# Nine shared weight buffers with the low half in place of the raw piece, and modulation gains spread by transposes

## The chip, the cores and the metric

The kernel runs on one core of one Trainium2 chip. The metric is the device time of one execution in microseconds (us), the median of several runs. Five engines work side by side, each in the order of its own program: TensorE (PE; its weight loads are shown apart, as PEld), VectorE (DVE), ScalarE (ACT), GpSimd (POOL), and SyncE (SP), which here only issues DMAs. They meet at semaphores alone. "Granted clock" is the share of full speed at which TensorE is allowed to run: it is either 1.00 or 0.50 in this trace.

## The reference

256 tokens of width 1024 go through two blocks of two layers each, all in float32. The first block has sparse attention, a gating branch, a gated feed-forward network and layer norms. The second is modulated: a vector `c` makes, through `ada_w`, six vectors for each layer, of which `g1` and `g2` (called gains here) multiply what a sublayer adds to the residual.

```python
def second_block(x, c, positions, ada_w, ada_b, norm_mix, norm_mlp, mlp_w1, mlp_w2, ...):
    cond = jax.nn.silu(c.astype(jnp.float32)).astype(x.dtype)
    for layer in range(DEPTH):
        mod = cond @ ada_w[layer] + ada_b[layer]
        sh1, sc1, g1, sh2, sc2, g2 = jnp.split(mod, 6, axis=-1)
        h = modulate(rms_norm(x, norm_mix[layer]), sh1, sc1)
        if layer % 2 == 0:
            y = even_mixer(h, ...)
        else:
            y = odd_mixer(h, ...)
        x = x + g1[:, None, :] * y
        h = modulate(rms_norm(x, norm_mlp[layer]), sh2, sc2)
        x = x + g2[:, None, :] * squared_relu_mlp(h, mlp_w1[layer], mlp_w2[layer])
    return x
```

## The kernel before, in words

**Weights.** All weight matrices lie in one array `W`, cut in 258 pieces of at most 128 partitions x 2048 float32 (1 MB); a list `seq` holds them in the order of use. 210 pieces are matmul weights. Each is loaded to one of three buffers `RAW`. ScalarE rounds it to the high half `WH` (line 1476, part `split`), VectorE subtracts to get the low half `WL` (line 1678), and TensorE makes each product as three: high x high, low times high activations, high times low activations (lines 1358 to 1360). `WH` and `WL` have three buffers each, a pair for a piece. So three pieces can be split ahead of the matmuls (`NPAIR`), and three loaded ahead of the splits (`NRAW`). The other 48 pieces are `ada_w_2`; VectorE reads them straight out of `RAW` and sums them into `ACC` (line 1737), in the slack of other work.

**When a piece is loaded.** SP issues the loads in the order of `seq`. Load n waits until `RAW` buffer n mod 3 is free: until VectorE has made the low half of piece n-3 (event `wl`), or has summed it (event `ada`). A split of a piece waits until it has landed, and until the last matmul of the piece that used the pair before (event `mm`).

**Order.** One Python pass writes a list of parts (`do(...)`), and each engine's program is that list with the other engines' parts left out. Generators (`linear`, `linear2`, `partial`, `weave`) place elementwise work between the slots of a matmul chunk; `advance` puts the next splits into the list wherever it is called. `busy(b, n)` (line 1343) issues n matmuls of constants: work whose result is thrown away, put ahead of a place where TensorE is to wait.

**Gains.** `modc` holds the modulation vectors as columns: 128 values down the partitions, one column per 128 channels. For the residual they are needed along the free dimension, the same in every partition, as `VG` (part of the tile `VEC`). Part `gain` makes 512 channels of it: VectorE multiplies the identity by four columns to get four diagonal blocks (line 2038, into `SQ` in the even layer and into `E` in the odd one), TensorE issues three filler matmuls and one fp32 matmul of ones by that buffer (line 1423), and ScalarE copies the result to `VG`. There are four gains in each layer of the second block, eight in all, woven between the matmul chunks of the mixer's first products.

Of the kernel before, what the change touches and what calls it, by code (L numbers as in the profile page):

```python
# [19 lines left out]
NRAW = 3  # L20
NPAIR = 3
# [157 lines left out]
def program(nc, W, xd, xTd, pTd, posd, pos2d, colvd, cstd, cstbd, vecd, sgwd, smalld, out):  # L179
    with ExitStack() as ctx:  # L180
# [35 lines left out]
        trig = sb("trig", [128, 4, 2, 40])  # L216
# [72 lines left out]
        for n, it in enumerate(seq):  # L289
            it["id"] = n  # L290
            it["freed"] = ("ada", (n, 3)) if it["name"] == "ada_w_2" else ("wl", n)
        cur = {"chunk": 0, "item": 0, "made": 0, "used": 0, "acc": 0, "sum": 0, "id": 0, "col": 0, "turn": 0, "buf": 0,
               "ada": None}
        pair_user = [None] * NPAIR
# [7 lines left out]

        def advance(most=NPAIR):
            while cur["item"] < len(seq) and most:
                it = seq[cur["item"]]
                if it["name"] == "ada_w_2":
# [3 lines left out]
                    do("ada", it, [] if it["a"] else acc_free[a])  # L310
                    if it["a"]:
# [36 lines left out]
        def linear(name, lhs, after, evac, touter=False, mid=None, guard=None, pad=(0, 0)):  # L348
# [5 lines left out]
            def slot(it, t):  # L354
# [3 lines left out]
                if t:  # L358
                    cur["used"] += 1

            if touter:
                assert len(its) <= NPAIR
# [31 lines left out]
        def linear2(name, lhs, after, evacs, mid, pad=(0, 0)):  # L394
# [13 lines left out]
            for t in range(2):  # L408
                if t:
                    ps[0][1], ps[1][1] = take(), take()  # L410
                for it in ia:
                    slot(it, 0, t)
                    if t:
                        cur["used"] += 1
# [8 lines left out]
            cur["used"] += 1  # L423
# [4 lines left out]
            cur["used"] += 1  # L428
# [9 lines left out]
        def partial(name, parts, ps, first, last, evac=None):  # L438
# [5 lines left out]
            def one(n, t):  # L444
# [4 lines left out]
                if t:  # L449
                    cur["used"] += 1  # L450
# [6 lines left out]
            else:  # L457
                assert len(its) <= NPAIR
# [46 lines left out]
        sq = {"free": []}  # L505
# [98 lines left out]

        advance(1)
# [274 lines left out]
        def gain(layer, k, hf, buf, box):  # L880
# [5 lines left out]
            do("gain", g, layer, k, hf, buf, b, mod_w[(layer, 3 * k + 2)] + box["free"], fr, list(vg_free[k]))  # L886
            box["free"] = [("gain_mm", g)]
# [37 lines left out]
        for i in range(2):  # L925
# [9 lines left out]
            if i == 0:  # L935
# [58 lines left out]
                gs = [lambda k=k, hf=hf: gain(0, k, hf, SQ[:, :], sq) for k in range(2) for hf in range(2)]  # L994
# [41 lines left out]
            else:  # L1036
# [13 lines left out]
                def turn_qk(c, t, base, lst):  # L1050
# [4 lines left out]
                gs = [lambda k=k, hf=hf: gain(1, k, hf, E[:, k, hf * 512:hf * 512 + 512], e_box[k])  # L1055
                      for k in range(2) for hf in range(2)]
# [185 lines left out]
        def sync_program(eng):  # L1242
            on = Waits(eng)

            def load(n):
                it = seq[n]
# [3 lines left out]
                eng.dma_start(RAW[:, n % NRAW, 0:w], W[it["off"]:it["off"] + 128 * w].rearrange("(p w) -> p w", p=128)  # L1250
                              ).then_inc(*landed(f"raw{n % NRAW}", n))

            for n in range(NRAW):
                load(n)
            eng.dma_start(X[:, :, :], xd[0].rearrange("(t p) d -> p t d", p=128)).then_inc(*landed("x", 0))
            for n in range(NRAW, len(seq)):
                load(n)
            for part, args in order:
                if part == "store":
                    t, after = args  # L1260
                    for e in after:
                        on.wait_ge(*at(*e))
                    eng.dma_start(out[0, tok(t), :], X[:, t, :]).then_inc(*landed(f"out{t}", 0))
# [900 lines left out]
```

## Time and profile before

| | |
|---|---|
| median of 3 runs | 1469.46 us (1466.57 to 1469.95) |
| the profiled execution's own time | 1465.74 us |
| its span, first to last instruction | 1463.9 us |
| mean granted clock | 0.980 |
| VectorE, ScalarE, GpSimd busy | 948.0, 657.1, 108.7 us |
| bytes read from HBM | 267.75 MB, 184 GB/s over the span |

How to read it: busy time is the time in which an engine has an instruction under way; TensorE's ends are modelled, and a matmul's shown duration overlaps the next one's, so its true pace is read from the distance of two starts. A wait is named by the instruction that waited and by what released it. Rows with "xN" stand for N instructions.

### The profile page before, as it was taken

How to read it: one execution, taken by the hardware profiler on the slowest of the kernel's cores; microseconds unless marked ns; L12 is line 12 of the kernel's file. 1: busy time of each engine (PE TensorE's matmuls, PEld its weight loads, DVE VectorE, ACT ScalarE, POOL GpSimd, SP SyncE). 2: the span in 40 equal slices, each digit the busy share in tenths (PEclk: the TensorE clock that was granted, in tenths of full speed). 3: DMA queues.
4: the chain of work that ended last, by engine and by line, in shares of the span. 5: the costliest groups of instructions: out<-in, count | busy, mean ns of one | idle time of the engine just before them, and what ended most of it. 6: DMA issues, size and time to landing. Idle time of an engine off the chain costs nothing.

```text
span 1463.9 us, 16616 instructions
## 1 busy us (share of the span) xinstructions
PE 1364.7 (93%) x6723; PEld 1111.9 (76%) x6723; DVE 948.0 (65%) x1257; ACT 657.1 (45%) x886; POOL 108.7 (7%) x156
## 2 busy tenths in 40 slices
PE   6899999999989999999799898999998978899998
PEld 5767888887867788887588776888876656688886
DVE  4856777766675677775566856867665775544444
ACT  4644533333554443333455444544435444454542
POOL 1010000000020000000222300000003130000000
PEclk9999999999999999999999999999999998999999
DMA  8505678763623688874143204776753330345551
GB/s 330 201 18 201 224 295 293 297 245 113 244 73 103 230 292 298 297 288 133 61 164 125 86 20 154 287 263 255 278 211 128 131 115 25 120 172 176 186 184 58
DMA packets 40236, 269.87 MB, mean 184 GB/s; under 512 B 4544, under 2 KB 4688, under 8 KB 11872
## 3 DMA queue, kind: packets, MB, share of 16 engines
q1 hardware_dynamic: 37712, 259.31, 49.3%
q0 software_dynamic: 2304, 8.46, 1.6%
q8 instruction: 53, 0.87, 0.2%
q10 hardware_dynamic: 144, 1.05, 0.2%
q14 instruction: 23, 0.19, 0.0%
HBM read 267.75 MB, written 1.05 MB: 184 GB/s over the span
## 4 chain that ended last, share of the span: by engine, by line
PE 72%; DVE 14%; ACT 6%; issue 3%; DMA 2%; POOL 2%; SPq 0%; DVEq 0%; ACTq 0%; POOLq 0%
PE ps L1358 21%; PE ps L1360 21%; PE ps L1359 21%; PE ps L1383 4%; DVE WL L1678 3%; DMA RAW<-W 2%; ACT WH L1476 2%; ACT E L1476 1%; PE ps L1371 1%; PE ps L1463 1%; POOL st L1282 1%; PE ps L1439 1%; DVE st L1872 1%; PE ps L1343 1%; ACT XTH L1476 1%
## 5 line engine op out<-in xcount | busy, mean ns | idle before, releaser
L1678 DVE TENSOR_TENSOR WL<-RAW,WH 128x2048 fp32r<-128x2048 f32 (+5 forms) x210 | 453.3, 2161 | 281.1 <-ACT WH L1476 280.9
L1358 PE MATMUL ps<-WH,XTH 128*128 128x512 f32 (+3 forms) x1176 | 459.3, 391 | 33.7 <-DVE XTL L1683 14.4
L1476 ACT ACTIVATE WH<-RAW 128x2048 fp32r<-128x2048 f32 (+5 forms) x210 | 379.9, 1810 | 245.8 <-PE ps L1360 217.1
L1360 PE MATMUL ps<-WH,XTL 128*128 128x512 f32 (+3 forms) x1176 | 447.6, 381 | 0.0
L1359 PE MATMUL ps<-WL,XTH 128*128 128x512 f32 (+3 forms) x1176 | 446.5, 380 | 0.0
L1358 PEld LDWEIGHTS ps<-WH,XTH 128*128 128x128 f32 x1176 | 222.3, 189 | 78.5 <-DVE XTL L1683 14.7
L1360 PEld LDWEIGHTS ps<-WH,XTL 128*128 128x128 f32 x1176 | 221.9, 189 | 38.6
L1359 PEld LDWEIGHTS ps<-WL,XTH 128*128 128x128 f32 x1176 | 222.6, 189 | 36.8 <-issue 1.9
L1358 PE MATMUL ps<-WH,HTH 128*128 128x512 f32 (+1 forms) x452 | 180.1, 398 | 3.2 <-DVE HTL L1759 3.2
L1359 PE MATMUL ps<-WL,HTH 128*128 128x512 f32 (+1 forms) x452 | 179.1, 396 | 0.0
L1360 PE MATMUL ps<-WH,HTL 128*128 128x512 f32 (+1 forms) x452 | 178.9, 396 | 0.0
L1737 DVE SCALAR_TENSOR_TENSOR ACC<-RAW,colv,ACC 128x512 f32<-128x512 f32 x168 | 126.1, 751 | 5.1
L1476 ACT ACTIVATE HTH<-ps 128x512 fp32r<-128x512 f32 (+1 forms) x58 | 32.1, 585 | 160.5 <-PE ps L1383 160.4
L1358 PEld LDWEIGHTS ps<-WH,HTH 128*128 128x128 f32 x452 | 86.2, 191 | 22.8 <-DVE HTL L1759 3.7
L1360 PEld LDWEIGHTS ps<-WH,HTL 128*128 128x128 f32 x452 | 86.2, 191 | 19.8
L1359 PEld LDWEIGHTS ps<-WL,HTH 128*128 128x128 f32 x452 | 86.4, 191 | 19.2
L1280 POOL TENSOR_SCALAR st<-st 128x1 f32<-128x1 f32 (+3 forms) x42 | 21.6, 513 | 1034.5 <-DVE st L1943 540.1
L1476 ACT ACTIVATE GB<-ps 128x512 f32<-128x512 f32 (+1 forms) x94 | 46.3, 499 | 88.3 <-PE ps L1360 88.2
L1476 ACT ACTIVATE E<-ps,st 128x128 f32<-128x128 f32 (+1 forms) x104 | 42.4, 420 | 79.8 <-DVE st L1882 79.8
L1343 PE MATMUL ps<-cstb 128*128 128x512 bf16 x283 | 78.1, 398 | 0.0
L1759 DVE TENSOR_TENSOR HTL<-ps,HTH 128x512 fp32r<-128x512 f32 x54 | 35.8, 687 | 37.7 <-ACT HTH L1476 37.7
L1282 POOL TENSOR_TENSOR st<-st,cst 128x1 f32<-128x1 f32 (+3 forms) x42 | 47.2, 1124 | 3.5
(177 smaller groups left out, 1063.5 us busy)
## 6 DMA issues: line engine op xcount, KB each, us to landing
RAW<-W SPq DMA_DIRECT2D x220, 1024.0 KB, 4.8
RAW<-W SPq DMA_DIRECT2D x7, 960.0 KB, 4.7
RAW<-W SPq DMA_DIRECT2D x6, 910.0 KB, 6.2
RAW<-W SPq DMA_DIRECT2D x9, 576.0 KB, 3.5
VEC<-vecd POOLq DMA_DIRECT2D x10, 512.0 KB, 6.0
RAW<-W SPq DMA_DIRECT2D x8, 512.0 KB, 3.4
RAW<-W SPq DMA_DIRECT2D x6, 546.0 KB, 4.4
GB<-xTd ACTq DMA_DIRECT2D x1, 1024.0 KB, 8.3
```

The lines of the kernel that those rows point to most:

```text
L1280: eng.tensor_scalar(x, x, scale, eps, ALU.mult, ALU.add).then_inc(*own.up())
L1282: eng.tensor_tensor(x, x, MH.to_broadcast([128, x.shape[1]]), ALU.pow).then_inc(*up("rsqrt", key))
L1343: eng.matmul(banks[b][:, :], identb, cstb[:, 0:512], start=True, stop=True)
L1358: eng.matmul(ps, xh, hi[:, j, c0:c0 + cw], start=first and j == 0, stop=False)
L1359: eng.matmul(ps, xh, lo[:, j, c0:c0 + cw], start=False, stop=False)
L1360: op = eng.matmul(ps, xl, hi[:, j, c0:c0 + cw], start=False, stop=last and j == n - 1)
L1371: op = eng.matmul(banks[b][:, q:q + 1], ACC[:, a, q * 128:q * 128 + 128], ones[:, 0:1], start=True, stop=True)
L1383: op = eng.transpose(banks[b][0:rows, j * 128:j * 128 + 128], src, ident)
L1476: return eng.activation(dst, src, f, **k)
L1678: eng.tensor_tensor(WL[:, p, 0:w], RAW[:, n % NRAW, 0:w], WH[:, p, 0:w].bitcast(F32), ALU.subtract).then_inc(*up("wl", n))
L1737: op = eng.scalar_tensor_tensor(out=ACC[:, a, :], in0=view[:, j, :], scalar=cond[:, kt:kt + 1], in1=ACC[:, a, :], op0=ALU.mult, op1=ALU.add)
L1759: eng.tensor_tensor(HTL[:, r2:r2 + 2, :], banks[b][:, :].rearrange("p (n q) -> p n q", n=2), HTH[:, r2:r2 + 2, :].bitcast(F32), ALU.subtra ...
```

## The change

It has two parts.

**Buffers.** `RAW`, `WH` and `WL` become one pool of nine buffers of the same size `WB` (seen as float32 under the name `RAW`). A load takes the buffer at the head of a queue of free ones, and so does the high half of a split; the low half is written over the raw piece itself. After the last matmul of a piece its two buffers go to the end of the queue with the event `mm`; an `ada_w_2` piece gives back its one with the event `ada`. The limits stay: three pairs, and three pieces loaded but not yet split. The loads, which SP had in a loop of their own, now stand in the common list of parts. `trig`, used once at the start, moves into `SQ`.

**Gains.** The diagonal on VectorE, the three fillers and the matmul of ones are gone. In their place TensorE transposes, four times, a column of `modc` that is read 128 times over (a step of 0), with the identity as the moving operand: each gives a block of 128 x 128 in which every row holds the 128 values.

```diff
-        RAW = sb("RAW", [128, NRAW, SLOT])
-        WH = sb("WH", [128, NPAIR, SLOT], F32R)
-        WL = sb("WL", [128, NPAIR, SLOT], F32R)
+        with nc.sbuf_tensor("RAW", [128, NBUF, SLOT], F32) as RAW:
+            pass
+        WB = sb("WB", [128, NBUF, SLOT], F32R)
...
-        trig = sb("trig", [128, 4, 2, 40])
+        trig = SQ[:, 0:320].rearrange("p (n t f) -> p n t f", n=4, t=2)
...
+        def loads(most=NBUF):
+            while cur["load"] < len(seq) and most and cur["load"] - cur["item"] < NBUF - 2 * cur["pairs"] and bufs:
+                it = seq[cur["load"]]
+                it["raw"], after = bufs.pop(0)
+                do("load", it, after)
+                cur["load"] += 1
+                most -= 1
+
+        def advance(most=NBUF):
+            loads()
+            while cur["item"] < cur["load"] and most:
                 it = seq[cur["item"]]
                 if it["name"] == "ada_w_2":
...
                     do("ada", it, [] if it["a"] else acc_free[a])
+                    bufs.append((it["raw"], [("ada", (it["id"], 3))]))
...
                 else:
-                    if cur["made"] - cur["used"] >= NPAIR:
+                    if cur["ahead"] >= cur["pairs"] or not bufs:
                         return
                     most -= 1
-                    p = it["pair"] = cur["made"] % NPAIR
-                    cur["made"] += 1
-                    do("split", it, pair_user[p])
-                    pair_user[p] = it["id"]
+                    cur["ahead"] += 1
+                    it["high"], after = bufs.pop(0)
+                    do("split", it, after)
                 cur["item"] += 1
+                loads()
+
+        def used(it):
+            cur["ahead"] -= 1
+            for b in (it["high"], it["raw"]):
+                bufs.append((b, [("mm", it["id"])]))
+            loads()
...
         def sync_program(eng):
...
-                if n >= NRAW:
-                    on.wait_ge(*at(*seq[n - NRAW]["freed"]))
+                for e in after:
+                    on.wait_ge(*at(*e))
...
-            def gain(g, layer, k, hf, buf, b, _, fr, __):
-                for e in fr:
-                    on.wait_ge(*at(*e))
-                busy(b, 3)
-                on.wait_ge(*at("diag", g))
-                eng.matmul(banks[b][:, :], ones, buf, start=True, stop=True).then_inc(*up("gain_mm", g))
+            def gain(g, layer, k, hf, b, after, fr, _):
+                for e in fr + after:
+                    on.wait_ge(*at(*e))
+                on.wait_ge(*at("cst", 0))
+                for j in range(4):
+                    c = 24 * k + 16 + hf * 4 + j
+                    op = eng.transpose(banks[b][:, j * 128:j * 128 + 128],
+                                       modc[:, layer, c:c + 1].to_broadcast([128, 128]), ident)
+                op.then_inc(*up("gain_mm", g))
...
-                eng.tensor_tensor(WL[:, p, 0:w], RAW[:, n % NRAW, 0:w], WH[:, p, 0:w].bitcast(F32), ALU.subtract
-                                  ).then_inc(*up("wl", n))
+                eng.tensor_tensor(WB[:, it["raw"], 0:w], RAW[:, it["raw"], 0:w], WB[:, it["high"], 0:w].bitcast(F32),
+                                  ALU.subtract).then_inc(*up("wl", n))
...
-            def gain(g, layer, k, hf, buf, b, after, _, __):
-                c0 = 24 * k + 16 + hf * 4
-                on.wait_ge(*at("cst", 0))
-                for e in after:
-                    on.wait_ge(*at(*e))
-                eng.tensor_tensor(buf.rearrange("p (a n) -> p a n", a=4), ident.unsqueeze(1).broadcast_to([128, 4, 128]),
-                                  modc[:, layer, c0:c0 + 4].unsqueeze(2).broadcast_to([128, 4, 128]), ALU.mult
-                                  ).then_inc(*up("diag", g))
```

TensorE's program at the first gain of the even layer before the change, between two chunks of `even_w_in_2` (`cstb` holds the constants of the fillers, `SQ` the diagonal):

```order
L1359 MATMUL ps<-WL,XTH 128x384
L1360 MATMUL ps<-WH,XTL 128x384
L1343 MATMUL ps<-cstb 128x512 x3
L1423 MATMUL ps<-SQ,cst 128x512
L1358 MATMUL ps<-WH,XTH 128x384
L1359 MATMUL ps<-WL,XTH 128x384
```

And the same place in the change (its lines have other numbers, and both halves are called `WB`):

```order
L1376 MATMUL ps<-WB,XTH 128x384
L1377 MATMUL ps<-WB,XTL 128x384
L1442 MATMUL ps<-cst,modc 128x128 x4
L1375 MATMUL ps<-WB,XTH 128x384
L1376 MATMUL ps<-WB,XTH 128x384
```

Three fillers and a matmul of 512 columns give way to four transposes of 128; nothing else moves on TensorE, here or at the seven other gains, and VectorE loses the eight diagonals and nothing more.

SP's program at its start, with the semaphores that each load waits for, before (`s_wl` is raised by VectorE's low half):

```order
L1250 DMA RAW<-W 128x1820
L1255 DMA X<-xd 128x2x1024
L1250 DMA RAW<-W 128x1092 [waits s_wl]
L1250 DMA RAW<-W 128x1820 [waits s_wl]
L1250 DMA RAW<-W 128x1092 [waits s_wl]
L1250 DMA RAW<-W 128x2048 [waits s_wl] x8
```

And in the change (`s_mm` is raised by TensorE's last matmul of a piece):

```order
L1266 DMA RAW<-W 128x1820
L1270 DMA X<-xd 128x2x1024
L1266 DMA RAW<-W 128x1092
L1266 DMA RAW<-W 128x1820
L1266 DMA RAW<-W 128x1092
L1266 DMA RAW<-W 128x2048 [waits s_mm] x8
```

The loads keep their order. The fourth to the sixth wait for nothing now, and from the seventh on a load waits for matmuls that are further back, in place of a low half that comes later. ScalarE's program, with all its splits, keeps its order and its waits.

## Rows read from the trace of the kernel before

**Rows 1.** The page, part 1: busy time, share of the span and instructions of each engine.
```profile
PE 1364.7 (93%) x6723; PEld 1111.9 (76%) x6723; DVE 948.0 (65%) x1257; ACT 657.1 (45%) x886; POOL 108.7 (7%) x156
```

**Rows 2.** Waits of TensorE: who <- whom: us in total, times, longest.
```profile
PE ps L1439 <- DVE selb L1860: 4.4, 2, 2.7
PE ps L1423 <- DVE E L2038: 2.6, 2, 1.3
PE ps L1358 <- DVE WL L1678: 2.4, 3, 1.1
...
PE ps L1423 <- DVE SQ L2038: 1.0, 1, 1.0
```

**Rows 3.** Stretches: length, busy PE, PEld, DVE, ACT, POOL, clock, DMA share, GB/s.
```profile
23.00:27.00 4.00, 4.00 (x26) 4.00 (x25) 1.94 (x4) 3.53 (x6) 2.24 (x5) 1.00 0.23 67
...
421.00:427.60 6.60, 5.05 (x20) 3.67 (x21) 4.04 (x10) 3.37 (x17) 1.15 (x1) 0.50 0.00 0
750.00:785.00 35.00, 33.96 (x181) 29.36 (x180) 30.58 (x42) 18.21 (x24) 9.28 (x8) 1.00 0.45 152
784.00:788.00 4.00, 3.61 (x33) 3.36 (x31) 1.45 (x3) 3.39 (x7) 0.00 (x0) 1.00 0.69 240
1125.00:1160.00 35.00, 32.36 (x135) 23.30 (x134) 27.49 (x34) 16.86 (x18) 11.27 (x8) 1.00 0.49 177
```

**Rows 4.** One line's instructions: the diagonals, ns min/median/max of one.
```profile
L2038 DVE TENSOR_TENSOR SQ<-cst,modc x4: 680/684/684, 759.2 to 778.7; 128x512 f32<-128x512 f32 x4
```

**Rows 5.** TensorE in order of time at the first gain: start, us, line, tiles.
```profile
759.62 0.82 PE L1343 MATMUL ps<-cstb 128*128 128x512 bf16 x3
760.28 1.02 PE L1423 MATMUL ps<-SQ,cst 128*128 128x512 f32 x2
...
761.32 0.34 PE L1359 MATMUL ps<-WL,XTH 128*128 128x384 f32 x1
761.49 0.34 PE L1360 MATMUL ps<-WH,XTL 128*128 128x384 f32 x1
```

**Rows 6.** TensorE in order of time at the eighth gain.
```profile
1154.75 0.82 PE L1343 MATMUL ps<-cstb 128*128 128x512 bf16 x3
...
1158.07 0.40 PE L1359 MATMUL ps<-WL,XTH 128*128 128x512 f32 x1
```

**Rows 7.** TensorE in order of time: eight transposes between weight matmuls.
```profile
946.08 1.03 PE L1383 MATMUL ps<-cst,GB 128*128 128x128 f32 x8
...
947.18 0.40 PE L1359 MATMUL ps<-WL,XTH 128*128 128x512 f32 x1
947.41 0.39 PE L1360 MATMUL ps<-WH,XTL 128*128 128x512 f32 x1
```

**Rows 8.** VectorE in order of time where the two stretches of gains end.
```profile
785.46 0.69 DVE L1751 COPY T<-ps 96x512 f32<-96x512 f32 x1 [1.39 <-PE ps L1383]
...
1164.38 0.69 DVE L1751 COPY T<-ps 128x512 f32<-128x512 f32 x1 [1.61 <-PE ps L1383]
```

**Rows 9.** SP in order of time: issue of the seventh load.
```profile
26.83 0.33 SPq L1250 DMA_DIRECT2D RAW<-W  x1
```

**Rows 10.** TensorE in order of time: the first piece's last matmul.
```profile
23.06 0.34 PE L1360 MATMUL ps<-WH,XTL 128*128 128x364 f32 x1
```

**Rows 11.** ScalarE in order of time: the seventh and eighth pieces.
```profile
36.66 1.92 ACT L1476 ACTIVATE WH<-RAW 128x2048 fp32r<-128x2048 f32 x1 [3.22 <-DMA RAW<-W]
40.09 1.92 ACT L1476 ACTIVATE WH<-RAW 128x2048 fp32r<-128x2048 f32 x1 [1.51 <-DMA RAW<-W]
```

**Rows 12.** VectorE in order of time: low half, first rotation.
```profile
42.04 2.29 DVE L1678 TENSOR_TENSOR WL<-RAW,WH 128x2048 fp32r<-128x2048 f32 x1 [1.14 <-ACT WH L1476]
44.24 0.23 DVE L1795 TENSOR_TENSOR SCR<-H,COS 128x80 f32<-128x80 f32 x1
```

**Rows 13.** TensorE in order of time behind those rotations, first and second layer.
```profile
49.08 0.63 PE L1383 MATMUL ps<-cst,H 128*128 128x128 f32 x4 [0.52 <-DVE MIX L1819]
...
393.19 1.65 PE L1404 MATMUL ps<-T 64*128 64x128 f32 x16 [0.56 <-DVE T L1751]
```

More of the change, by code:

```diff
@@ L19 @@
 SLOT = 2048
-NRAW = 3
-NPAIR = 3
+NBUF = 9
 DFF = 2816
@@ L290, in program @@
             it["id"] = n
-            it["freed"] = ("ada", (n, 3)) if it["name"] == "ada_w_2" else ("wl", n)
-        cur = {"chunk": 0, "item": 0, "made": 0, "used": 0, "acc": 0, "sum": 0, "id": 0, "col": 0, "turn": 0, "buf": 0,
+        cur = {"chunk": 0, "item": 0, "load": 0, "ahead": 0, "pairs": 3, "acc": 0, "sum": 0, "id": 0, "col": 0, "turn": 0, "buf": 0,
                "ada": None}
-        pair_user = [None] * NPAIR
+        bufs = [(n, []) for n in range(NBUF)]
         acc_free = [[], []]
@@ L358, in slot @@
                 if t:
-                    cur["used"] += 1
+                    used(it)
             if touter:
-                assert len(its) <= NPAIR
+                assert len(its) <= cur["pairs"]
                 advance()
@@ L422, in linear2 @@
                 slot(ib[0], 1, t)
-            cur["used"] += 1
+            used(ib[0])
             yield
@@ L427, in linear2 @@
                 slot(ib[1], 1, t)
-            cur["used"] += 1
+            used(ib[1])
             for t in range(2):
@@ L449, in one @@
                 if t:
-                    cur["used"] += 1
+                    used(it)
             if evac is None:
@@ L457, in partial @@
             else:
-                assert len(its) <= NPAIR
+                assert len(its) <= cur["pairs"]
                 advance()
@@ L504, in program @@
         scr = {"free": [("cstb", 0)]}
-        sq = {"free": []}
+        sq = {"free": [("trig", 0)]}
         def weave(gen, steps):
@@ L601, in normalised @@
             return dict(n=nh, done=done)
+        loads(3)
+        do("load_x")
         advance(1)
@@ L878, in program, with gain @@
         vg_free, vg_w = [list(vec_free[0]), list(vec_free[0])], [[], []]
-        def gain(layer, k, hf, buf, box):
+        def gain(layer, k, hf):
             assert len(mod_w[(layer, 3 * k + 2)]) == 2
@@ L885, in gain @@
             b, fr = take()
-            do("gain", g, layer, k, hf, buf, b, mod_w[(layer, 3 * k + 2)] + box["free"], fr, list(vg_free[k]))
-            box["free"] = [("gain_mm", g)]
+            do("gain", g, layer, k, hf, b, mod_w[(layer, 3 * k + 2)], fr, list(vg_free[k]))
             vg_w[k].append(("gain", g))
@@ L993, in program @@
                                             SIN[:, t, 8:40:2], sm[nm], ww[t], E[:, n, :], e_box[n], mr[n, t])
-                gs = [lambda k=k, hf=hf: gain(0, k, hf, SQ[:, :], sq) for k in range(2) for hf in range(2)]
+                gs = [lambda k=k, hf=hf: gain(0, k, hf) for k in range(2) for hf in range(2)]
                 run(weave(dils(4, 5, 0), [[mch[0, 0][0], mch[1, 0][0]], [gs[0], mch[0, 0][1], mch[0, 1][0]],
@@ L1054, in program @@
                 e_box = [{"free": list(e_free[0])}, {"free": list(e_free[1])}]
-                gs = [lambda k=k, hf=hf: gain(1, k, hf, E[:, k, hf * 512:hf * 512 + 512], e_box[k])
-                      for k in range(2) for hf in range(2)]
+                gs = [lambda k=k, hf=hf: gain(1, k, hf) for k in range(2) for hf in range(2)]
                 run(weave(chain(linear2("odd_w_in_2", "x", xt_w, [put_H("odd", c, c * 512, c * 512 + 512, dw[c])
@@ L1478, in scalar_program, with split @@
             eng.dma_start(GBT, xTd.rearrange("p (k n) -> p k n", k=8)).then_inc(*landed("xT", 0))
-            def split(it, user):
-                n, p, w = it["id"], it["pair"], it["n"] * it["w"]
-                on.wait_ge(*at(f"raw{n % NRAW}", n))
-                if user is not None:
-                    on.wait_ge(*at("mm", user))
-                act(WH[:, p, 0:w], RAW[:, n % NRAW, 0:w], ACT.Copy).then_inc(*up("wh", n))
+            def split(it, after):
+                n, w = it["id"], it["n"] * it["w"]
+                on.wait_ge(*at(f"raw{it['raw']}", n))
+                for e in after:
+                    on.wait_ge(*at(*e))
+                act(WB[:, it["high"], 0:w], RAW[:, it["raw"], 0:w], ACT.Copy).then_inc(*up("wh", n))
             def x0(t):
@@ L1647, in qk_sq, with gain @@
                 act(sqt, x, ACT.Square).then_inc(*up("qk_sq", key))
-            def gain(g, layer, k, hf, buf, b, _, __, after):
+            def gain(g, layer, k, hf, b, _, __, after):
                 on.wait_ge(*at("gain_mm", g))
```

40 lines of the change are left out of this document (18 added, 22 removed).

## The prediction

> **What bounds the kernel now.** I read the page's busy times first: TensorE is busy in 93% of the span, VectorE in 65% [rows 1]. A shown matmul overlaps the next one, so the share alone proves little; the distance of starts does. Inside a chunk three-pass matmuls start 0.17 us apart at 384 columns [rows 5] and 0.23 us apart at 512 [rows 7], with nothing between them: TensorE is the bound there, and whatever it no longer does comes off the time unless another engine is close behind. Second, its waits [rows 2]: for the low half of weights it waits 2.4 us in all, so a freer weight pipeline has little to give as such; for the gains' diagonals it waits 2.6 + 1.0 = 3.6 us. Third, the stretches in which the gains lie, 750 to 785 us (four of the even layer) and 1125 to 1160 us (most of the four of the odd one) [rows 3]: TensorE is busy 33.96 and 32.36 of 35 us, VectorE 30.58 and 27.49. So TensorE leads there, and VectorE is the one close behind.
>
> **The gains, TensorE's part.** I time one old gain from the start of the fillers to the start that the next weight matmul would have had at its usual pace, which is the second weight matmul's start less one distance (the first shows its wait for the fp32 matmul in its own length). At the first gain [rows 5]: 761.32 − 0.17 − 759.62 = 1.53 us, without a wait: three fillers, then one fp32 matmul of 512 columns. At the eighth [rows 6]: 1158.07 − 0.23 − 1154.75 = 3.09 us, with the longest of the waits for a diagonal, 1.3 [rows 2]. Read so, the eight cost 1.53, 1.84, 2.79, 1.52, 1.51, 3.10, 1.59 and 3.09 us: 17.0 in sum. By the grouped rows it is 8 × 1.53 + 3.6 = 15.8; the missing 1.1 is what a late start adds to the pipeline's refill. I take 17.0 and keep 15.8 as a bound.
>
> What comes instead is four fp32 transposes of 128 columns. Eight of that form, between the same kind of weight matmuls, took 947.18 − 0.23 − 946.08 = 0.87 us [rows 7]: 0.11 each, 0.44 for four, 3.5 for all eight gains. The difference is 17.0 − 3.5 = 13.5 us. The new wait that the transposes bring, for `modc`, moves from VectorE to TensorE; the diagonal that had it ran at 759.2 us [rows 4], before the fillers were over, so it costs nothing. What the trace doesn't have is a stationary operand that reads one column 128 times. Upper bound: its four passes cost what the old fp32 matmul cost for the same 512 columns, from its start to the next one's pace, 761.15 − 760.28 = 0.87 us [rows 5]; that takes 8 × 0.43 = 3.4 us off the saving. Lower bound: the 0.44 itself, since a repeated column gives TensorE no fewer columns to pass than any other. I take 0.44, as form and size are those of [rows 7] and only the address step differs.
>
> The trace has 0.11 us for each of the transposes. By the Trainium skill (TensorE: Matmul & The Clock Gate, section on LDWEIGHTS) a load takes columns / 1.2 ns, whatever it reads, so an estimate by the page is 107 ns for 128 columns; it names no penalty for a step of 0, so it would leave the sum at 13.5, where the upper bound gives 10.1.
>
> **The gains, VectorE's part.** Eight diagonals of 0.68 us go [rows 4]: 2.7 us in each stretch. That counts only if VectorE becomes late. Two facts: in the even stretch TensorE saves 1.53 + 1.84 + 2.79 + 1.52 − 4 × 0.44 = 5.9 us, VectorE has 35 − 30.58 = 4.4 us idle and loses 2.7 of work: 7.1 of room [rows 3, 4]. In the odd one TensorE saves 9.29 − 1.76 = 7.5, VectorE has 7.5 idle and loses 2.7: 10.2 of room. And at the end of both the next copy of VectorE waited for TensorE, 1.39 and 1.61 us [rows 8]. So VectorE can follow; it could take up to 1 us of the even stretch, as its idle time isn't all in the right place. No other engine's order moves there; ScalarE has half of its time free.
>
> **The buffers.** There are nine buffers of 1 MB before and after. From the seventh load on, a load used to wait for a low half three pieces back; now it waits for the matmuls of a piece some six back, done earlier. The pieces land earlier, but TensorE waited only 2.4 us for low halves [rows 2], so I count a gain only where a late load reached TensorE through the splits. That is at the start. DMA's share is 0.23 from 23 to 27 us [rows 3], since SP issues the seventh load at 26.83 [rows 9]; the first piece's last matmul, for which it now waits, ends at 23.06 + 0.34 = 23.40 [rows 10]. So 3.4 us earlier. The seventh split waited 3.22 us for DMA, the eighth 1.51 [rows 11]; both waits go, so the eighth starts at least 1.5 us sooner, and with it VectorE's low half, which waited for it, and the rotations that stand right behind [rows 12]. TensorE's stalls behind those rotations are 0.52 and 0.56 us, with the refill 0.68 and 0.72 [rows 13], and I take 1.35 of these 1.40. The same stall in the second layer (393.19) [rows 13] should go by the same means, 0.7. Bounds: nothing at all, if other waits take their place at once; 3.2 + 0.7 + 2.4 = 6.3, if the whole wait of the seventh split comes through to the end of the layer's attention, where TensorE waits up to 2.7 us for VectorE's `selb` [rows 2], and the waits for low halves all go. I take 2.05.
>
> Loads four to six are issued some 10 us earlier. They stand in one queue behind the first three and X, so they overtake nothing.
>
> **Sum.** 13.5 + 2.05 = 15.5 us. The profiled execution took 1465.74 us for a span of 1463.9; less 15.5 it is 1450.2. The median of the runs shown stands 3.7 us above it (1469.46), so the time as measured is 1469.46 − 15.5 = 1454.0. The terms' own bounds: least 15.8 − 8 × 0.87 = 8.8, less 1 for VectorE, 7.8, so 1461.7; most 13.5 + 6.3 = 19.8, so 1449.7. The three runs spread over 3.4 us, so the forecast's own range is 1448 to 1462.
>
> **Rivals.**
> (B) *VectorE becomes the bound in both stretches.* For: 30.58 of 35 us busy in the even one [rows 3], and the diagonals came late at half of the gains [rows 2], so VectorE runs behind TensorE in places. Against: the copies at the ends wait for TensorE [rows 8]. Then only VectorE's relief counts: 8 × 0.68 + 2.05 = 7.5 us, 1462.
> (C) *The earlier loads give much more.* For: SP's late loads leave DMA idle in places. DMA's share is 0.45 and 0.49 in the gains' stretches [rows 3]. If both waits of [rows 11] came off in full (4.7 us), with the second layer's 0.7, the 2.4 for low halves and 1 more that no row names, the gain would be 22.3: 1447. Against: between them and the end stand TensorE's stalls of 0.68 and 0.72 us, which is all that it can take back there itself.
> (D) *The buffers give nothing*, because the splits come where their place in the program and the pair limit put them: 13.5 alone, 1456. It lies inside the range.
> (E) *Slower: the granted clock falls behind the gains.* TensorE's clock is 0.50 from 421.0 to 427.6 us, where it is busy 5.05 of 6.60 us [rows 3]; full speed is 2.4 GHz, so it is at 1.2 there. The fillers go at all eight gains. If each were followed by one such stretch, half of 6.6 us would be lost eight times, 26.4 us: 1454 + 26.4 = 1480. It decides from 15.5 / 8 = 1.9 us lost, or 3.9 us at low clock, behind each. Against: without fillers and waits TensorE is busier there, not idler; and from 784 to 788 us, where it makes the 32 transposes of keys and queries in a row, the clock stays at 1.00 [rows 3].
> For that rule stands the Trainium skill (TensorE: Matmul & The Clock Gate, section PE-mode transpose): the full clock "doesn't engage" for transposes, which don't count as busy. This trace disagrees for 3.5 us in a row, and here only 0.44 us of them stand between weight matmuls; no run yet shows them in the place of fillers.
>
> **How the numbers follow.** Forecast with (D) 0.80, (B) 0.11, (C) 0.04, (E) 0.03, and 0.02 for a change that moves nothing because something outside the gains' stretches sets the time. The range from 1447 to 1463 holds the first three, but for tails that I put at 0.1 together. About 0.3%, 4.4 us, is what a measurement of this kernel can tell from no change. The forecast, (C) and (D) are well beyond it; of (B) most is, since its 7.5 us could shrink by half if VectorE is late by more. So faster 0.92, within 0.3% 0.05, slower 0.03.
>
> **What would show it.** In the changed kernel's trace: at each gain the distance from the last weight matmul to the next one's pace is 0.4 to 0.5 us, with no wait named before the transposes. If it is 0.8, the repeated column is dear. The weight matmuls behind them keep their 0.17 and 0.23 us apart and clock 1.00; else (E). The copies of VectorE at the ends of both stretches still wait for TensorE, and the even stretch ends about 6 us, the odd one 7.5 us nearer to its beginning; else (B). The seventh load is issued near 23.4 us, the seventh split doesn't wait for DMA, and TensorE's stalls at 49 and 52 us are gone; else (D). I'd be wrong in kind if TensorE's waits elsewhere grew by what it saved here.

## The result and the profile after

| | before | changed |
|---|---|---|
| median of all runs taken together | 1468.01 us (4 runs, 1466.08 to 1469.95) | 1452.71 us (4 runs, 1450.07 to 1456.84) |
| ratio | | 0.9899, 95% interval 0.9882 to 0.9917 |
| profiled execution, its span | 1465.74, 1463.9 us | 1450.07, 1448.3 us |
| mean granted clock of it | 0.980 | 0.981 |

The forecast was 1454.0 us by a saving of 15.5. The two spans differ by 15.6 us, the medians by 15.3. Measured again beside before on the same chip, the changed kernel gave a ratio of 0.9892 (0.9874 to 0.9909).

The page of the changed kernel, parts 1 and 2 (busy time, share and instructions of each engine; granted clock in 40 slices):

```profile
PE 1352.1 (93%) x6683; PEld 1111.1 (77%) x6715; DVE 943.2 (65%) x1249; ACT 656.9 (45%) x886; POOL 113.7 (8%) x156
...
PEclk9999999999999999999999999999999988999999
```

TensorE's busy time fell by 12.6 us and VectorE's by 4.8 against [rows 1]: 8 diagonals of 0.68 make 5.4. The share of TensorE is what it was, since the span fell with it.

TensorE at the first and at the eighth gain, in order of time (start, us; lines have moved by 17, and both halves are `WB` now):

```profile
757.90 0.60 PE L1442 MATMUL ps<-cst,modc 128*128 128x128 f32 x4
758.25 0.42 PE L1375 MATMUL ps<-WB,XTH 128*128 128x384 f32 x1
758.51 0.34 PE L1376 MATMUL ps<-WB,XTH 128*128 128x384 f32 x1
...
1141.59 0.60 PE L1442 MATMUL ps<-cst,modc 128*128 128x128 f32 x4
1141.94 0.48 PE L1375 MATMUL ps<-WB,XTH 128*128 128x512 f32 x1
1142.26 0.39 PE L1376 MATMUL ps<-WB,XTH 128*128 128x512 f32 x1
```

Read as in the prediction: 758.51 − 0.17 − 757.90 = 0.44 us, and 1142.26 − 0.23 − 1141.59 = 0.44 us, where [rows 5, 6] give 1.53 and 3.09. No wait is named before the transposes.

The waits of TensorE in the changed kernel (who <- whom: us in total, times, longest):

```profile
PE ps L1460 <- DVE selb L1881: 4.4, 2, 2.7
...
PE ps L1375 <- DVE WB L1699: 2.4, 3, 1.1
```

The rows of [rows 2] for the diagonals are gone; those for the low half and for `selb` stand as they were. The pool did nothing for TensorE's waits for weights.

The start: SP's seventh load, ScalarE's seventh and eighth piece, and VectorE's first rotation in the changed kernel:

```profile
23.56 1.82 SPq L1266 DMA_DIRECT2D RAW<-W  x2
```
```profile
33.46 1.91 ACT L1497 ACTIVATE WB<-RAW 128x2048 fp32r<-128x2048 f32 x1
38.18 1.92 ACT L1497 ACTIVATE WB<-RAW 128x2048 fp32r<-128x2048 f32 x1 [2.81 <-PE ps L1377]
```
```profile
42.34 0.24 DVE L1816 TENSOR_TENSOR SCR<-H,COS 128x80 f32<-128x80 f32 x1
```

The load is issued 3.3 us sooner than in [rows 9]; both waits for DMA of [rows 11] are gone, and the eighth split now waits for the matmuls of the pair before; the rotation starts 1.9 us sooner than in [rows 12]. TensorE behind it, first and second layer:

```profile
48.26 0.60 PE L1400 MATMUL ps<-cst,H 128*128 128x128 f32 x4
...
50.23 1.65 PE L1421 MATMUL ps<-T 64*128 64x128 f32 x16
...
390.97 1.65 PE L1421 MATMUL ps<-T 64*128 64x128 f32 x16
```

The waits of [rows 13] are gone. VectorE's copies at the ends of the even and the odd stretch, which waited 1.39 and 1.61 us for TensorE in [rows 8]:

```profile
778.71 1.28 DVE L1772 COPY T<-ps 96x512 f32<-96x512 f32 x2
```
```profile
1148.57 0.69 DVE L1772 COPY T<-ps 128x512 f32<-128x512 f32 x1
```

Neither waits for TensorE any more, so VectorE has used up its room there. TensorE doesn't wait for VectorE at these ends either: it waits 0.82 and 0.93 us for a copy of ScalarE, where before it waited 0.82 and 0.94.

To find where the time came from, I compare when the same weight matmul starts in both traces, and call the difference the lead. All 4932 weight matmuls have a counterpart.

| place | forecast | lead gained |
|---|---|---|
| up to the first scores (before at 53 us) | 1.35 | 1.44 |
| second layer's scores (395 us) | 0.7 | 0.77 |
| from there to the first gain | 0 | −0.48 |
| the four gains of the even layer (lead 1.73 to 7.55) | 5.9 | 5.82 |
| between them and the odd layer's gains | 0 | 0.67 |
| the four gains of the odd layer (lead 8.22 to 15.81) | 7.5 | 7.59 |
| from there to the end | 0 | −0.20 |
| sum | 15.5 | 15.61 |

The three rows whose forecast is 0 hold steps of 0.3 to 2.7 us of both signs. The largest stand where one trace has a stretch at granted clock 0.50 and the other hasn't, or has it at another place (before's matmuls from 1086 to 1114 us: the lead rises by 2.7 and falls by 2.3). That the three rows cancel to 0.01 us is luck.

### The profile page after: what moved, and what is told of

It is laid out like the page before. It is cut to its first block, busy times and chain, and to the rows that moved or that the text cites. A ratio compares the mean times of both kernels' runs of the same rounds, so it can differ in the third digit from the quotient of the medians.

```text
span 1448.3 us, 16560 instructions
## 1 busy us (share of the span) xinstructions
PE 1352.1 (93%) x6683; PEld 1111.1 (77%) x6715; DVE 943.2 (65%) x1249; ACT 656.9 (45%) x886; POOL 113.7 (8%) x156
## 4 chain that ended last, share of the span: by engine, by line
PE 78%; DVE 11%; ACT 5%; issue 2%; POOL 2%; DMA 1%; DVEq 0%; ACTq 0%; POOLq 0%
PE ps L1375 23%; PE ps L1377 23%; PE ps L1376 23%; PE ps L1400 4%; DVE WB L1699 2%; ACT E L1497 1%; PE ps L1484 1%; PE ps L1388 1%; POOL st L1299 1%; ACT WB L1497 1%; PE ps L1460 1%; DVE st L1893 1%; PE ps L1360 1%; ACT XTH L1497 1%; DVE st L1961 1%
## 5 line engine op out<-in xcount | busy, mean ns | idle before, releaser
L1699 DVE TENSOR_TENSOR WB<-RAW,WB 128x2048 fp32r<-128x2048 f32 (+5 forms) x210 | 453.3, 2161 | 271.7 <-ACT WB L1497 271.5
L1375 PE MATMUL ps<-WB,XTH 128*128 128x512 f32 (+3 forms) x1176 | 457.3, 389 | 33.3 <-DVE XTL L1704 14.0
L1497 ACT ACTIVATE WB<-RAW 128x2048 fp32r<-128x2048 f32 (+5 forms) x210 | 379.8, 1809 | 237.5 <-PE ps L1377 223.1
L1377 PE MATMUL ps<-WB,XTL 128*128 128x512 f32 (+3 forms) x1176 | 447.9, 381 | 0.0
L1376 PE MATMUL ps<-WB,XTH 128*128 128x512 f32 (+3 forms) x1176 | 447.2, 380 | 0.0
L1375 PEld LDWEIGHTS ps<-WB,XTH 128*128 128x128 f32 x1176 | 222.7, 189 | 75.7 <-DVE XTL L1704 14.0
L1377 PEld LDWEIGHTS ps<-WB,XTL 128*128 128x128 f32 x1176 | 222.5, 189 | 38.7
L1376 PEld LDWEIGHTS ps<-WB,XTH 128*128 128x128 f32 x1176 | 223.0, 190 | 34.8
L1375 PE MATMUL ps<-WB,HTH 128*128 128x512 f32 (+1 forms) x452 | 179.3, 397 | 3.2 <-DVE HTL L1780 3.2
L1376 PE MATMUL ps<-WB,HTH 128*128 128x512 f32 (+1 forms) x452 | 178.5, 395 | 0.0
L1377 PE MATMUL ps<-WB,HTL 128*128 128x512 f32 (+1 forms) x452 | 178.5, 395 | 0.0
L1375 PEld LDWEIGHTS ps<-WB,HTH 128*128 128x128 f32 x452 | 85.9, 190 | 22.7 <-DVE HTL L1780 3.7
L1377 PEld LDWEIGHTS ps<-WB,HTL 128*128 128x128 f32 x452 | 85.8, 190 | 19.6
L1376 PEld LDWEIGHTS ps<-WB,HTH 128*128 128x128 f32 x452 | 86.0, 190 | 19.1
```

What stands on the lines that cost most here:

```text
L1375: eng.matmul(ps, xh, hi[:, j, c0:c0 + cw], start=first and j == 0, stop=False)
L1376: eng.matmul(ps, xh, lo[:, j, c0:c0 + cw], start=False, stop=False)
L1377: op = eng.matmul(ps, xl, hi[:, j, c0:c0 + cw], start=False, stop=last and j == n - 1)
L1497: return eng.activation(dst, src, f, **k)
L1699: eng.tensor_tensor(WB[:, it["raw"], 0:w], RAW[:, it["raw"], 0:w], WB[:, it["high"], 0:w].bitcast(F32), ALU.subtract).then_inc(*up("wl", n))
```

## Experiments

All ran beside before; the ratio is to before. The column "at 0.980" is explained under the clock and the runs' spread.

| kernel | ratio (95%) | median, runs | mean clock of the runs | at 0.980 |
|---|---|---|---|---|
| transposes alone | 0.9941 (0.9919 to 0.9962) | 1459.1 (6) | 0.976 | 1455.6 |
| nine buffers alone | 0.9985 (0.9975 to 0.9994) | 1465.4 (11) | 0.979 | 1464.2 |
| changed, loads at the old pace | 0.9924 (0.9903 to 0.9944) | 1455.1 (6) | 0.979 | 1454.7 |
| changed, diagonals kept unread | 0.9928 (0.9914 to 0.9942) | 1456.8 (5) | 0.978 | 1455.2 |
| nine buffers, old gains without fillers | 0.9989 (0.9979 to 0.9998) | 1467.7 (10) | 0.980 | 1466.9 |
| changed, three fillers put back | 0.9917 (0.9900 to 0.9933) | 1456.7 (4) | 0.981 | 1457.6 |
| changed, 20 transposes a gain | 1.0004 (0.9991 to 1.0017) | 1470.0 (10) | 0.977 | 1466.8 |
| the same with a full stationary tile | 0.9991 (0.9982 to 1.0001) | 1467.2 (10) | 0.978 | 1466.3 |
| changed, fewer fillers | 0.9893 (0.9877 to 0.9910) | 1451.2 (5) | 0.969 | |
| changed, no filler at all | 0.9952 (0.9937 to 0.9967) | 1460.8 (7) | 0.948 | |
| changed, fewer fillers at chosen places | 0.9842 (0.9826 to 0.9857) | 1445.6 (5) | 0.981 | 1446.6 |
| changed, once more | 0.9892 (0.9874 to 0.9909) | 1451.7 (6) | 0.980 | 1453.1 |

### The transposes alone

The kernel before with the new `gain` on TensorE; `RAW`, `WH`, `WL` and the loads' waits as before.

```diff
-                busy(b, 3)
-                on.wait_ge(*at("diag", g))
-                eng.matmul(banks[b][:, :], ones, buf, start=True, stop=True).then_inc(*up("gain_mm", g))
+                for j in range(4):
+                    c = 24 * k + 16 + hf * 4 + j
+                    op = eng.transpose(banks[b][:, j * 128:j * 128 + 128],
+                                       modc[:, layer, c:c + 1].to_broadcast([128, 128]), ident)
```

> The kernel before with the gains' transposes alone; the three pools and the load waits stay as before. Theory (the gains are 13.5 of the 15.5 us): 13.5 us below before, ratio 0.9908, each gain 0.44 us on TensorE; TensorE's stalls near 49 and 52 us and at 393 us stay. Rival (VectorE follows too slowly unless pieces come earlier): under 10 us, with VectorE's copies at the ends of the two stretches no longer waiting for TensorE.

Measured: 0.9941, 8.7 us, short of what was expected (0.9908 lies outside the interval). Both signs named for the rival are there: it is under 10 us, and VectorE's copies at the ends of the two stretches (783.91 and 1153.81 us) wait for TensorE no longer. Yet TensorE doesn't wait for VectorE there, but 0.82 and 0.94 us for ScalarE as in before, so the rival isn't what took the time. In the trace the gains gave what was forecast: the lead over before rises from −3.49 to 2.34 us over the even layer's four and from 2.99 to 10.58 over the odd layer's, 13.4 in sum. TensorE in order of time at one of them, and behind the first layer's rotations:

```profile
763.11 0.60 PE L1422 MATMUL ps<-cst,modc 128*128 128x128 f32 x4
763.47 0.42 PE L1356 MATMUL ps<-WH,XTH 128*128 128x384 f32 x1
763.73 0.34 PE L1357 MATMUL ps<-WL,XTH 128*128 128x384 f32 x1
```
```profile
48.95 0.63 PE L1381 MATMUL ps<-cst,H 128*128 128x128 f32 x4 [0.49 <-DVE MIX L1820]
...
51.55 1.65 PE L1402 MATMUL ps<-T 64*128 64x128 f32 x16 [0.56 <-DVE T L1752]
```

0.44 us a gain, and the old stalls. The rest, 5.7 us, was lost outside, in parts that this kernel shares with before, most of it at granted clock 0.50: this trace has 76 us of it, before's 60 and the changed kernel's 56. Its six runs reach from 1452.75 to 1463.10, with mean clocks from 0.982 to 0.971; the fastest lies 14 us under before's median beside it, 1466.98, and 12 under before's fastest. So what the transposes save in place is shown; whether this kernel draws a low clock more often than the others, or six runs fell so, stays open.

### The nine buffers alone

The changed kernel with the old gains: diagonal on VectorE (into `SQ` or `E`), three fillers, matmul of ones.

> The changed kernel with the gains as before (diagonal, three fillers, matmul of ones): the nine buffers alone. Theory: 2 us below before (ratio 0.9986, hard to tell from none by the times); in the trace the lead over before is 1.3 us behind the first layer's rotations and 0.75 more in the second layer, nothing elsewhere. Rival (the pool makes nothing): lead within 0.5 us all through. Rival (the pool helps the diagonals too): more than 4 us.

```profile
48.80 1.03 PE L1362 MATMUL ps<-cstb 128*128 128x512 bf16 x4
49.80 1.65 PE L1423 MATMUL ps<-T 64*128 64x128 f32 x16
```
```profile
759.08 0.82 PE L1362 MATMUL ps<-cstb 128*128 128x512 bf16 x3
759.73 1.02 PE L1443 MATMUL ps<-SQ,cst 128*128 128x512 f32 x2
760.19 0.74 PE L1377 MATMUL ps<-WB,XTH 128*128 128x384 f32 x1
760.77 0.34 PE L1378 MATMUL ps<-WB,XTH 128*128 128x384 f32 x1
```

TensorE in order of time: no stall before the scores, and an old gain of 760.77 − 0.17 − 759.08 = 1.52 us. The lead steps up by 1.56 us up to the first scores and by 0.8 in the second layer; the gains' stretches add nothing. The ratio, 0.9985, is 2.2 us. That is as expected. The two profiled spans differ by 0.6 us alone, since this trace loses 2.6 us between the two steps, at 80 and at 140 us, where its stretches at 0.50 stand elsewhere than before's.

### The changed kernel with the loads at their old pace

```diff
                 it["raw"], after = bufs.pop(0)
+                n = cur["load"] - 3
+                if n >= 0:
+                    after = after + [("ada", (n, 3)) if seq[n]["name"] == "ada_w_2" else ("wl", n)]
```

> The changed kernel, but each load waits besides for the low half (or the sum) of the piece three back, as before: nine buffers in name, the old pace of the loads. Theory (the small gain is the loads' earlier issue): 2 us slower than the changed kernel, ratio to before 0.991; TensorE's stalls near 49, 52 and 393 us are back. Rival (it comes from the splits or the place of the low half): as the changed kernel, ratio 0.9895, without those stalls.

```profile
27.00 3.04 SPq L1269 DMA_DIRECT2D RAW<-W  x2
```
```profile
49.24 0.63 PE L1403 MATMUL ps<-cst,H 128*128 128x128 f32 x4 [0.18 <-DVE MIX L1843]
...
51.84 1.65 PE L1424 MATMUL ps<-T 64*128 64x128 f32 x16 [0.56 <-DVE T L1775]
```

The seventh load is issued at 27.00 us again (SP's row), and TensorE stalls again behind the rotations. The lead of the changed kernel over this one grows by 1.0 us there and is 1.6 at the first scores, where this kernel is no further than before: the first layer's gain comes from the loads' issue. In the second layer the stall did not come back. There ScalarE's split still waits 1.80 us for DMA (2.47 in before, 0 in the changed kernel), so the piece is late but by 0.7 us less than in before, and the stall was no longer than that. Why it lands sooner with the waits of before is open. The ratio, 0.9924 beside 0.9892 to 0.9899, is 4 to 5 us more than the changed kernel's, and at equal clock it is 1.6 (1454.7 and 1453.1 in the table); the intervals of the two overlap, so the times alone don't tell this from no difference.

### The diagonals kept, unread

VectorE makes all eight diagonals as before, into `SQ` and `E`; TensorE doesn't wait for them.

> The changed kernel with the eight diagonals still made on VectorE, where nobody reads them. Theory (TensorE leads, VectorE's relief is worth nothing): as the changed kernel, within 1 us, ratio 0.99. Rival (VectorE is the bound of the two stretches): 8 x 0.68 = 5.4 us slower, ratio 0.9935, and at the ends of both stretches TensorE waits for VectorE.

TensorE in order of time at the end of the even layer's stretch, this kernel and the changed one:

```profile
781.75 1.05 PE L1402 MATMUL ps<-cst,GB 128*96 128x128 f32 x8 [0.81 <-DVE GB L1822]
784.43 1.13 PE L1462 MATMUL ps<-T 96*128 96x128 f32 x8 [1.63 <-DVE T L1774]
```
```profile
779.05 1.04 PE L1400 MATMUL ps<-cst,GB 128*96 128x128 f32 x8
780.91 1.13 PE L1460 MATMUL ps<-T 96*128 96x128 f32 x8 [0.82 <-ACT T L1497]
```

My expectation was wrong, and the trace shows less than the rival's price of 5.4 us. With the diagonals VectorE ends the even stretch late: TensorE waits 0.81 + 1.63 us for it where the changed kernel waits 0.82 for ScalarE's copy, and the lead of the changed kernel grows by 1.8 us. Behind that wait the weight matmuls start 0.32 us apart instead of 0.17 for 3.4 us (granted clock 0.50), another 1.6. In the odd layer 0.6 is lost, which makes 4.0 us in all. The ratio, 0.9928 against 0.9892 to 0.9899, says 4 to 5, and its interval (0.9914 to 0.9942) holds the rival's 0.9935. So VectorE's relief is a condition of the even layer's 5.8 us: with 4.4 us idle in [rows 3] and no diagonal gone, it could not follow TensorE by 5.9.

### The old gain without its fillers

```diff
-                busy(b, 3)
                 on.wait_ge(*at("diag", g))
                 eng.matmul(banks[b][:, :], ones, buf, start=True, stop=True).then_inc(*up("gain_mm", g))
```

> Nine buffers, the gain by diagonal and fp32 matmul as before, but without its three fillers. Theory: a gain costs 0.87 us where the diagonal is ready, and where TensorE waited for it before it waits the three fillers' 0.66 us longer, so the four that waited stay as they were and the other four save 0.66: about 2.6 us below the nine buffers alone, ratio 0.997. Rival (the fillers are the cost): 8 x 0.66 = 5.3 us, ratio 0.995. Rival (the fillers held the clock): slower than before, with the granted clock below 1.00 behind the gains.

TensorE's waits for diagonals, with the fillers (nine buffers alone) and without:

```profile
PE ps L1443 <- DVE E L2058: 2.7, 2, 1.3
...
PE ps L1443 <- DVE SQ L2058: 1.0, 1, 1.0
```
```profile
PE ps L1442 <- DVE E L2057: 4.1, 2, 2.1
...
PE ps L1442 <- DVE SQ L2057: 2.8, 3, 1.7
```

5.3 us of fillers went and 3.2 us of waits came, which leaves 2.1 to win; yet the time is 0.9989, no better than with the fillers. In the odd layer the trace has two stretches at 0.50 behind these waits, from 1142.9 and from 1159.9 us, 3.4 us each, which before hasn't, and the lead over the nine buffers alone, whose trace hasn't them either, falls by 2.3 us there. That looks like the third of the theories, that the fillers held the clock, but it is one execution. The ten runs' mean clock is 0.980, against 0.979 for the nine buffers alone with fillers, and the kernel isn't slower than before. So it isn't shown that the fillers held the clock here; why the 2.1 us didn't come stays open. What is shown is that taking off the fillers alone brings nothing; the transposes take the wait away with them.

### Three fillers put back ahead of the transposes

> The changed kernel with the three fillers put back ahead of the transposes. Theory (fillers are plain TensorE time): 8 x 0.66 = 5.3 us slower than the changed kernel, ratio to before 0.993, a gain costs 1.10 us. Rival (the transposes lower the clock and fillers hide it): no slower.

Measured 0.9917, 2 to 4 us over the changed kernel's where 5.3 were expected (0.993 lies just inside the interval), and 4.5 at equal clock; in the trace this kernel falls behind the changed one by 0.66 at each of the eight gains, 5.3 in sum. A filler ahead of ready work is TensorE time at full price. The transposes take 0.44 us, as in the changed kernel.

### Twenty transposes a gain, of a repeated column and of a full tile

```diff
-                for j in range(4):
+                for j in [0, 1, 2, 3] * 5:
```

and, in the second kernel, `ident` in place of the repeated column (the gains' values are not computed).

> The changed kernel with each gain's four transposes of the repeated column made five times over (20 in place of 4). Theory: 16 x 0.109 = 1.75 us more a gain, 14.0 us more in all, which takes back almost all that was gained (ratio 0.999), clock at 1.00 through 2.2 us of transposes. Rival (a repeated column is dearer than the 0.109 us of the others once they run in a row, or the clock falls): more than 20 us.

> As the run with 20 transposes a gain, but the stationary operand is the identity, a full tile of 128 columns, in place of one column read 128 times (so the gains' values are not computed). Theory: the load is as long either way, same time within 1 us. Rival (the step of 0 has a price): faster than with the repeated column by 160 times that price in sum (0.01 us each would be 1.3 us).

```profile
760.49 2.35 PE L1442 MATMUL ps<-cst,modc 128*128 128x128 f32 x20
762.60 0.42 PE L1375 MATMUL ps<-WB,XTH 128*128 128x384 f32 x1
762.86 0.34 PE L1376 MATMUL ps<-WB,XTH 128*128 128x384 f32 x1
```
```profile
758.85 2.35 PE L1442 MATMUL ps<-cst 128*128 128x128 f32 x20
760.95 0.42 PE L1375 MATMUL ps<-WB,XTH 128*128 128x384 f32 x1
761.21 0.34 PE L1376 MATMUL ps<-WB,XTH 128*128 128x384 f32 x1
```

762.86 − 0.17 − 760.49 = 2.20 us with the repeated column, 2.19 with the full tile: 0.110 us each, and the address step has no price. The two medians differ by 2.8 us, more than the expected 1 and the way that the rival had it; but over the eight gains both traces lose the same 14.1 us against the changed kernel, and at equal clock the two lie 0.5 apart. And the granted clock of the whole stretch with 80 of these transposes in it, in the kernel of the first fence:

```profile
758.00:785.00 27.00, 27.00 (x187) 26.83 (x186) 22.10 (x32) 12.31 (x16) 8.96 (x7) 1.00 0.44 154
```

1.00. The Trainium skill (TensorE: Matmul & The Clock Gate, section PE-mode transpose) says that the full clock doesn't engage for transposes; for up to 2.2 us of them in a row between weight matmuls, this trace disagrees. No run here has transposes alone for longer than the 3.5 us of [rows 3]. By the ratios the two kernels are 13 to 16 us over the changed one; the 128 added transposes are 14.1.

### Fewer fillers

The changed kernel's trace has fillers at 68 places. At about half of them, what TensorE does next was ready before the fillers began.

```diff
-                    turns(units[k - 1], pads[k - 1] if k <= len(pads) else 2)
+                    turns(units[k - 1], pads[k - 1] if k <= len(pads) else 0)
...
-                attention(units, 0.125, fill, (2, 3, 3, 3, 1, 1), pads=(2, 2, 12, 6))
+                attention(units, 0.125, fill, (2, 3, 3, 3, 1, 1), pads=(0, 0, 0, 6))
```

(and `pad=(0, 3)` to `(0, 0)` at `w_ple_gate`, 4 to 2 ahead of the scores)

> The changed kernel with fewer fillers at places where, in its trace, what TensorE does next was ready before the fillers began: none ahead of attention's transposes of E but where eight or six are asked for (before two, once twelve), none ahead of the gating products' second tile, two in place of four ahead of the scores. The fillers that go there took 14 to 15 us in sum. Theory (a filler in front of work that is ready is plain TensorE time): 8 to 14 us below the changed kernel, ratio to before 0.981 to 0.985. Rival (they hold the granted clock where ScalarE's exponentials leave TensorE gaps): under 4 us or slower, with longer stretches at 0.50 in the attention parts.

> The changed kernel without any filler. Those that run before ready work took about 15 us; the others fill waits and cost nothing, so without a clock there would be 15 us to gain. Theory (the long groups keep the clock up behind waits): the mean granted clock falls below 0.97, and the time is over that of the run with fewer fillers, by some 10 us or more. Rival (fillers do nothing for the clock): ratio to before 0.98, as with fewer fillers.

Stretches (length, busy PE, PEld, DVE, ACT, POOL, clock, DMA share, GB/s) of the changed kernel in its second run, of the one with fewer fillers, and of the one with none:

```profile
750.00:810.00 60.00, 59.07 (x366) 57.55 (x367) 46.43 (x67) 37.01 (x66) 19.72 (x16) 1.00 0.44 151
810.00:870.00 60.00, 51.77 (x346) 41.48 (x350) 39.32 (x98) 24.99 (x81) 8.97 (x9) 0.97 0.10 36
1180.00:1232.00 52.00, 38.27 (x240) 28.68 (x240) 31.96 (x63) 19.89 (x58) 8.98 (x8) 0.90 0.05 20
```
```profile
750.00:810.00 60.00, 59.18 (x375) 58.02 (x374) 48.15 (x74) 34.18 (x67) 20.51 (x16) 1.00 0.44 150
810.00:870.00 60.00, 50.00 (x295) 39.52 (x294) 34.71 (x91) 24.86 (x81) 8.20 (x8) 0.83 0.05 18
1180.00:1232.00 52.00, 36.14 (x200) 28.86 (x199) 29.96 (x59) 19.37 (x58) 8.65 (x8) 0.74 0.01 3
```
```profile
810.00:870.00 60.00, 47.11 (x279) 40.92 (x278) 37.61 (x97) 24.30 (x79) 10.27 (x10) 0.77 0.09 36
1180.00:1232.00 52.00, 33.58 (x195) 27.13 (x192) 33.18 (x69) 21.14 (x64) 8.99 (x8) 0.77 0.11 41
```

The theory lost: 0.9893, as the changed kernel. Its lead over the changed kernel's first trace is 6.35 us at 805 us. Then it falls by 4.6 up to 860 us and by 1.9 from 1170 to 1220, where the clock is 0.83 and 0.74 instead of 0.97 and 0.90 (0.84 in the first trace), and by 1.7 at 915 us, where only this trace is at 0.50; at the end it is 1.1 us behind. From 750 to 810 us, where TensorE is busy 59 of 60 us, taking fillers off left the clock at 1.00. Without any filler the mean clock is 0.948, 152 us stand at 0.50, and the kernel is 8 to 9 us slower than the changed one.

### Fewer fillers at chosen places

The same edits, but the default of two stays in the second sparse attention of block two, and the differential attention keeps all of its fillers.

> The changed kernel with fewer fillers in the first three attentions, ahead of the gating product and ahead of the scores, but with all that stand in the second sparse attention of block two and in the differential one, where the run before lost its lead at clock 0.50 (from 832 to 850 us and from 1184 to 1218). Theory (fillers cost where TensorE has little idle time around them, and hold the clock where it has much): the lead of about 6 us that the run before had at 805 us stays to the end: 5 to 6 us below the changed kernel, ratio to before 0.986, low clock for about 55 to 60 us in all. Rival (the clock takes it back elsewhere): ratio 0.989 to 0.990.

> The changed kernel itself once more, beside the run with fewer fillers on the same chip. Theory: ratio to before 0.990, as at first, with runs some 6 us apart that go with the mean granted clock, about 0.7 us for each 0.001 as over all runs so far.

```profile
750.00:810.00 60.00, 59.18 (x374) 58.02 (x373) 48.18 (x72) 33.40 (x63) 20.49 (x16) 1.00 0.44 149
810.00:870.00 60.00, 50.35 (x324) 39.29 (x328) 36.89 (x95) 25.87 (x83) 8.19 (x8) 0.94 0.06 19
```

0.9842 (0.9826 to 0.9857) beside 0.9892 (0.9874 to 0.9909) for the changed kernel: 1445.61 us, faster than both kernels of this case, with 55 us at 0.50, as in the changed kernel's second run (53). Its lead over that run is 5.5 us at 812 us and 4.4 at the end. The places were chosen with the trace of the run before in hand, so this shows that a better choice exists, not a rule that finds it. By the medians it is 6.1 us below the changed kernel, where 5 to 6 were expected. The lead grew most where TensorE has few gaps: by 1.5 us from 400 to 500 us, where it is busy 23.3 of 25 us from 425 to 450, and by 1.8 from 790 to 812 us, where it is busy 21.9 of 22. From 68 to 100 us, at 26.5 of 32, taking fillers off moved it by −0.7.

### The clock and the runs' spread

Each run lists its mean granted clock. A least squares fit over the 147 runs here (all but those without fillers), with a constant for each kernel and one slope for all, gives 0.74 us for each 0.001 of clock, with 1.2 us left over; "at 0.980" is a kernel's constant there. By it the parts add up: gains 11.3, buffers 2.7, both 13.8 us below before's 1466.9. The traces, compared matmul by matmul, have 13.4 and 2.1 to 2.4. By the plain ratios the parts don't add up: 0.9941 × 0.9985 = 0.9926, and both together measured 0.9899 and 0.9892. The fit puts the 4 to 5 us between them down to the clock that the runs drew; a cause for that isn't shown.

## Why the prediction was right

- *TensorE bounds the gains' stretches.* Right. The lead grows at the gains by what TensorE no longer does, and three fillers put back cost their full length.
- *17.0 us of old gains, 0.44 us for four transposes, 13.5 saved.* Right: 0.44 at the first and the eighth, and 5.82 + 7.59 = 13.41 over the two stretches. The unknown, the step of 0, costs nothing.
- *VectorE can follow.* Right for this change, as its own diagonals go, but with less to spare than forecast. The sign that was named, copies at both ends that still wait for TensorE, failed: they wait no longer, while TensorE waits for VectorE at neither end. The prediction had the relief in its room (4.4 us of idle time and 2.7 of relief against 5.9), but when I wrote the expectation for the diagonals kept I dropped the relief; that run showed its worth, 1.8 us of waiting and 1.6 us of clock.
- *The buffers: 2.05 us, at two places.* Right: 1.30 and 0.8 in the changed kernel, 2.2 by the times for the buffers alone. In the first layer the loads' issue is shown to be the cause; in the second it isn't settled.
- *Rivals.* (B), VectorE as the bound, was half true in one stretch, and only with the diagonals there. (C) is refuted by the buffers alone, 2.2 us, and by the wait for low halves, which is still 2.4 us. (D) is refuted by the buffers alone, whose interval (0.9975 to 0.9994) leaves out 1, and by the two steps of their lead. (E), a falling clock behind the transposes, did not happen: 1.00 with 4 and with 20 a gain. But fillers do hold the clock elsewhere (a mean of 0.948 without any, against 0.980); whether they did at the old gains isn't settled.
- *The run to run range.* 1448 to 1462 as the likeliest case's own range was fair: the changed kernel's ten runs reach from 1450.07 to 1458.23.

## What to carry to other kernels

Where one engine streams without gaps, time its instructions by the distance of starts, count what a change takes from it, and check that the next engine has at least that much room; here that gave 15.5 us for 15.6. A wait with fillers ahead of it is best removed together with the fillers: here the fillers alone, taken off while the wait was there, gave nothing (0.9989 against 0.9985). Remove a filler whose successor was ready before it began if TensorE is busy without gaps around it (59 of 60 us here). Where TensorE has gaps (52 of 60), taking such fillers off cost more than it gave here, so test it there before you do.

## What the runs showed of the hardware

- An fp32 transpose of 128 columns costs 0.110 us in a row of 20, with a stationary column read 128 times as with a full tile; an fp32 matmul of 512 columns by ones costs 0.87 us [rows 5].
- Two executions of one program differ by up to 10 us in 1450 on this core (the transposes alone: 1452.75 and 1463.10), and most of it goes with the mean granted clock, 0.74 us for each 0.001.
- One wait of 1.63 us after one of 0.81 was followed by 3.4 us at 0.50, in a stretch that otherwise stood at 1.00.
